# Modulation of the second block's rows: from VectorE before the transposes to ScalarE in the turned form

## The reference, cut to what matters

```python
def hybrid_layer(x, c_act, norm_g, w_ada, b_ada, w_in, w_out, pos):
    mod = c_act @ w_ada + b_ada
    shift, scale, gate = jnp.split(mod, 3, axis=-1)
    h = rms_norm(x, norm_g) * (1.0 + scale[:, None, :]) + shift[:, None, :]
    proj = h @ w_in
    ...                       # retention and stick-breaking attention of proj -> y
    return x + gate[:, None, :] * (y @ w_out)
```

## Time and profile before

| | us |
|---|---|
| median of 3 runs (1628.9 to 1629.87) | 1628.91 |
| the profiled execution, device time | 1628.01 |
| its span, first to last instruction | 1626.2 |
| TensorE busy in the span | 1583.9 (97%) |
| VectorE busy | 1069.6 (66%) |
| ScalarE busy | 728.7 (45%) |
| granted TensorE clock, mean over the span | 0.995 |

### The profile page before, as it was taken

How to read it: one execution, slowest core, us unless ns; L and a number is a source line. 1 busy time by engine, 2 the same in 40 slices (tenths; PEclk the granted TensorE clock), 3 DMA queues, 4 the chain that set the end, 5 groups by cost and what they waited for, 6 DMA issues and landing times.

```text
span 1626.2 us, 20209 instructions
## 1 busy us (share of the span) xinstructions
PE 1583.9 (97%) x8388; PEld 1327.8 (82%) x8388; DVE 1069.6 (66%) x1454; ACT 728.7 (45%) x874; POOL 48.9 (3%) x89
## 2 busy tenths in 40 slices
PE   7999999999989999999999999999999999999998
PEld 5898888888878888888888888788888878887986
DVE  5784776747666776575766746957767577556744
ACT  4545444433443443345444443454444344554452
POOL 1100000000000000000000000000100000000000
PEclk9999999999999999999999999999999999999999
DMA  8752466654424766452466654423766636433530
GB/s 268 257 184 77 156 227 251 241 224 177 160 78 169 281 224 252 149 208 83 164 240 237 257 197 163 155 79 127 272 257 233 229 133 225 145 129 117 207 117 26
DMA packets 45035, 299.89 MB, mean 184 GB/s; under 512 B 5444, under 2 KB 5700, under 8 KB 11280
## 3 DMA queue, kind: packets, MB, share of 16 engines
q1 hardware_dynamic: 38736, 278.48, 46.3%
q0 software_dynamic: 5776, 19.01, 3.8%
q10 hardware_dynamic: 432, 1.11, 0.2%
HBM read 296.20 MB, written 2.65 MB: 184 GB/s over the span
## 4 chain that ended last, share of the span: by engine, by line
PE 87%; DVE 8%; issue 2%; DMA 2%; ACT 1%; POOL 0%; SPq 0%; POOLq 0%; DVEq 0%; ACTq 0%
PE psum L925 25%; PE psum L927 25%; PE psum L926 25%; DVE w_low L1421 3%; PE psum L948 3%; PE psum L1139 2%; PE psum L1004 2%; DMA w_raw<-in_weights 2%; PE psum L1151 1%; PE psum L1065 1%; PE psum L1119 1%; PE psum L1203 1%; DVE arena L1703 1%; DVE work L1645 0%; DVE top L1642 0%
## 5 line engine op out<-in xcount | busy, mean ns | idle before, releaser
L925 PE MATMUL psum<-w_high,xt_high 128*128 128x512 f32 (+2 forms) x1472 | 576.5, 392 | 13.8 <-DVE w_low L1421 4.0
L1421 DVE TENSOR_TENSOR w_low<-w_raw,w_high 128x2048 fp32r<-128x2048 f32 x241 | 546.6, 2271 | 51.0 <-ACT w_high L1248 49.6
L1248 ACT ACTIVATE w_high<-w_raw 128x2048 fp32r<-128x2048 f32 x241 | 458.8, 1905 | 255.3 <-DMA w_raw<-in_weights 153.0
L927 PE MATMUL psum<-w_high,xt_low 128*128 128x512 f32 (+2 forms) x1472 | 566.7, 385 | 0.0
L926 PE MATMUL psum<-w_low,xt_high 128*128 128x512 f32 (+2 forms) x1472 | 565.8, 384 | 0.0
L925 PEld LDWEIGHTS psum<-w_high,xt_high 128*128 128x128 f32 x1472 | 278.7, 189 | 71.2 <-DVE w_low L1421 6.3
L927 PEld LDWEIGHTS psum<-w_high,xt_low 128*128 128x128 f32 x1472 | 278.4, 189 | 55.9
L926 PEld LDWEIGHTS psum<-w_low,xt_high 128*128 128x128 f32 x1472 | 279.0, 190 | 51.3
L1714 DVE TENSOR_TENSOR arena<-arena,psum 128x256 f32<-128x256 f32 x88 | 36.9, 420 | 205.5 <-ACT arena L1339 205.0
L925 PE MATMUL psum<-w_high,ht_high 128*128 128x512 f32 x352 | 140.8, 400 | 0.0
L927 PE MATMUL psum<-w_high,ht_low 128*128 128x512 f32 x352 | 137.5, 391 | 0.0
(11 more groups left out here) (225 smaller groups left out, 1605.3 us busy)
## 6 DMA issues: line engine op xcount, KB each, us to landing
w_raw<-in_weights SPq DMA_DIRECT2D x263, 1024.0 KB, 4.8
norm_params<-in_ln_g POOLq DMA_DIRECT2D x8, 512.0 KB, 4.3
norm_params<-in_ln_b POOLq DMA_DIRECT2D x8, 512.0 KB, 5.7
kv_outside<-arena POOLq DMA_DIRECT2D x3, 512.0 KB, 5.1
mem_kv<-kv_outside POOLq DMA_DIRECT2D x3, 512.0 KB, 3.6
norm_params<-mods_outside POOLq DMA_DIRECT2D x3, 512.0 KB, 5.8
x_rows<-in_x SPq DMA_DIRECT2D x2, 512.0 KB, 8.8
w_raw<-in_weights SPq DMA_DIRECT2D x2, 512.0 KB, 6.3
```

Of the source, the lines that this page charges most:

```text
L925: e.matmul(dst, a_hi, b_hi, start=first, stop=False)
L927: return e.matmul(dst, a_lo, b_hi, start=False, stop=last)
L1248: e.activation(K.w_hi[:, g % RING, 0:w], K.w_raw[:, r, 0:w], ACT.Copy).then_inc(K.high.hit(t), 1)
L1421: e.tensor_tensor(K.w_lo[:, s, 0:w], K.w_raw[:, r, 0:w], K.w_hi[:, s, 0:w].bitcast(F32), ALU.subtract).then_inc(K.taken.hit(t), 1)
```

## The change

- `modulate` moves to ScalarE and only scales the row by r: two copies of 512 columns with the scale column (semaphore `scaled`). In turned form a column of x is a partition, so gain and shift are then columns of 128 values. ScalarE's `xt` for ("sin", layer) makes, per group, four Identity activations of 128x128 with a bias and a scale column into `rows_turned`, waits for them, and rounds that to xt_high; VectorE's xt_low reads `rows_turned`. The others' `xt` are as before.
- `rms` squares in two halves of 512 columns, each behind its own half of x, and the scale 1/1024 goes into the square.
- gain and shift are loaded as columns (4 KB in runs of 4 bytes, four DMAs for the two layers) into a free buffer, so the waits of layer 1's load and of the decay's load go.
- The last down product of row block 1 in the last feed-forward is issued in two parts (one chunk of the depth each, 6 matmuls): part, group 0 of the turned rows 0, part, group 1. The `high` and `low` steps around it are put in another order.
- In layer 1, rows 1 are turned one product earlier (behind the fourth). In the output projection, rows 0 of the next layer are turned behind the second product of row block 1, not the third, and add_gated comes ahead of `split` in `last`.

```diff
@@ -199,12 +199,16 @@
...
-    def gemm(self, t, rb, half, gen, ring, use, kind="block", prompt=False):
+    def gemm(self, t, rb, half, gen, ring, use, kind="block", prompt=False, part=None):
+        if part == 0:
+            self.add("gemm", Gemm(t, rb, half, gen, ring, use, kind, part))
+            return
         for r in range(RB) if kind in BOTH else (rb,):
...
         self.last[t] = rb
-        self.add("gemm", Gemm(t, rb, half, gen, ring, use, kind))
+        self.add("gemm", Gemm(t, rb, half, gen, ring, use, kind, part))
         self.used[t] = self.used.get(t, 0) + 1
...
@@ -512,23 +516,29 @@
...
             for step in steps:
+                if rb and step == FF_STEPS - 1 and layer == LAST:
+                    down(step, t[step], rb, True, 0)
+                    self.xt(("sin", 0), 0, (0,))
+                    down(step, t[step], rb, True, 1)
+                    self.xt(("sin", 0), 0, (1,))
+                    self.ahead()
+                    continue
                 down(step, t[step], rb, True)
...
                         turn(FF_STEPS - 1)
-                elif step == FF_STEPS - 1:
-                    if layer == LAST:
-                        self.next_rows(layer, 0)
                 elif layer == LAST:
                     self.last_downs(step)
-                else:
+                elif step < FF_STEPS - 1:
                     if step == FF_STEPS - 2:
...
             if rb and layer == LAST:
+                self.low()
+                self.ahead()
                 self.low()
...
@@ -543,13 +553,12 @@
...
-        if step == FF_STEPS - 3:
+        if step == FF_STEPS - 4:
+            self.ahead()
+        elif step == FF_STEPS - 3:
+            self.add("rms", (0, 0))
+            self.add("modulate", (0, 0))
             self.low()
-            self.add("rms", (0, 0))
-            self.ahead()
-            self.add("modulate", (0, 0))
-        else:
-            self.ahead()
...
@@ -818,7 +827,12 @@
...
             self.on()
-        self.group([proj(0), proj(1)], gen, [[self.split] * 3 + [rotations(0), rows], [self.on] * 3 + [rotations(1), self.on]],
+        def rows_rotations():
+            late()
+            rotations(0)()
+        first = [rotations(0), rows] if layer == 0 else [rows_rotations, self.on]
+        self.group([proj(0), proj(1)], gen, [[self.split] * 3 + first, [self.on] * 3 + [rotations(1), self.on]],
                    layer == 0, proj(2))
...
@@ -869,19 +883,21 @@
...
         def turned():
-            self.low()
             if layer + 1 < DEPTH_2:
                 self.xt(("sin", layer + 1), 0)
-            else:
+            self.split()
+        def third():
+            if layer + 1 == DEPTH_2:
                 self.add("final", 0)
...
         def last():
+            added(3)
             self.split()
-            added(3)
         self.group([("w_out_2", layer, h * BLK, "half", sums(h)) for h in range(2)], mix,
-                   [[self.split, self.split, first, second], [self.split, self.split, turned, last]], True)
+                   [[self.split, self.split, first, second], [self.split, turned, third, last]], True)
...
@@ -995,7 +1011,7 @@
...
         elif stage == "sin":
-            pe.wait_ge(*K.modulated.at((j.gen[1], rb, g)))
+            pe.wait_ge(*K.scaled.at((j.gen[1], rb, g)))
             src = K.rows2[:, rb, :]
...
@@ -1014,12 +1030,12 @@
...
             pe.wait_ge(*K.tr.out(plan.ff_turn[j.gen[1], j.half]))
-            for h in range(2):
-                for c in range(2):
-                    left = [v[:, c, rb * P:rb * P + P] for v in (K.ht_hi[j.half % 4], K.ht_lo[j.half % 4])]
-                    w = c * D + h * BLK
-                    m = products(e, psum[:, K.wide.place(j.use) + h, :], left[0], left[1], hi[:, w:w + BLK],
-                                 lo[:, w:w + BLK], first and c == 0, last and c == 1)
+            parts = (0, 1) if j.part is None else (j.part,)
+            for h, c in ((h, c) for h in range(2) for c in parts):
+                left = [v[:, c, rb * P:rb * P + P] for v in (K.ht_hi[j.half % 4], K.ht_lo[j.half % 4])]
+                w = c * D + h * BLK
+                m = products(e, psum[:, K.wide.place(j.use) + h, :], left[0], left[1], hi[:, w:w + BLK],
+                             lo[:, w:w + BLK], first and c == 0, last and c == 1)
         else:
...
@@ -1253,9 +1270,20 @@
...
         act.wait_ge(*K.turned.at(j.use))
-        e.activation(hi[:, 4 * j.g:4 * j.g + 4, j.rb * P:j.rb * P + P],
-                     psum[:, K.tr.place(j.use), :].rearrange("p (c s) -> p c s", s=P),
-                     ACT.Copy).then_inc(K.xt_high.hit(j.use), 1)
+        src = psum[:, K.tr.place(j.use), :].rearrange("p (c s) -> p c s", s=P)
+        at = (slice(None), slice(4 * j.g, 4 * j.g + 4), slice(j.rb * P, j.rb * P + P))
+        if j.gen[0] == "sin":
+            act.wait_ge(*K.ld_gain2.at(j.gen[1]))
+            act.wait_ge(*K.ld_shift.at(j.gen[1]))
+            shift, gain = K.mod_cols[j.gen[1]]
+            for c in range(4):
+                k = 4 * j.g + c
+                m = e.activation(K.rows_turned[j.g][:, c, :], src[:, c, :], ACT.Identity, bias=shift[:, k:k + 1],
+                                 scale=gain[:, k:k + 1])
+            m.then_inc(K.modulated.hit(j.use), 1)
+            act.wait_ge(*K.modulated.at(j.use))
+            src = K.rows_turned[j.g]
+        e.activation(hi[at], src, ACT.Copy).then_inc(K.xt_high.hit(j.use), 1)
...
@@ -1356,12 +1384,21 @@
...
         layer, rb = j
-        if layer == 0:
-            act.wait_ge(*K.biased.at((("ln2", LAST), rb, 1)))
-        else:
-            act.wait_ge(*K.gated.at((layer - 1, rb, 1)))
-        e.activation(K.rows2[:, rb, :], K.x[:, rb, :], ACT.Square,
-                     accum_out=K.expsum[:, rb, 0:1]).then_inc(K.squared.hit(j), 1)
+        for n in range(2):
+            cols = slice(n * BLK, n * BLK + BLK)
+            act.wait_ge(*(K.gated.at((layer - 1, rb, n)) if layer else K.biased.at((("ln2", LAST), rb, n))))
+            m = e.activation(K.rows2[:, rb, cols], K.x[:, rb, cols], ACT.Square, scale=D ** -0.5,
+                             accum_out=K.expsum[:, rb, n:n + 1])
+        m.then_inc(K.squared.hit(j), 1)
+    def modulate(j):
+        layer, rb = j
+        act.wait_ge(*K.inverse_root.at((("rms", layer), rb)))
+        act.wait_ge(*K.squared.at(j))
+        for n in range(2):
+            cols = slice(n * BLK, n * BLK + BLK)
+            e.activation(K.rows2[:, rb, cols], K.x[:, rb, cols], ACT.Copy,
+                         scale=K.rstd[:, rb, 0:1]).then_inc(K.scaled.hit((layer, rb, n)), 1)
...
@@ -1444,8 +1481,10 @@
...
         v.wait_ge(*K.xt_high.at(j.use))
-        e.tensor_tensor(lo[at], psum[:, K.tr.place(j.use), :].rearrange("p (c s) -> p c s", s=P), hi[at].bitcast(F32),
-                        ALU.subtract).then_inc(K.tr.sem(j.use), 1)
+        src = psum[:, K.tr.place(j.use), :].rearrange("p (c s) -> p c s", s=P)
+        if j.gen[0] == "sin":
+            src = K.rows_turned[j.g]
+        e.tensor_tensor(lo[at], src, hi[at].bitcast(F32), ALU.subtract).then_inc(K.tr.sem(j.use), 1)
...
@@ -1755,20 +1794,8 @@
...
         v.wait_ge(*K.squared.at(j))
-        e.tensor_scalar(K.rstd[:, rb, 0:1], K.expsum[:, rb, 0:1], 1.0 / D, EPS_2, ALU.mult,
+        e.tensor_scalar(K.rstd[:, rb, 0:1], K.expsum[:, rb, 0:1], K.expsum[:, rb, 1:2], EPS_2, ALU.add,
                         ALU.add).then_inc(K.variance.hit((("rms", layer), rb)), 1)
-    def modulate(j):
-        layer, rb = j
-        v.wait_ge(*K.inverse_root.at((("rms", layer), rb)))
-        for h in range(2):
-            row = K.rows2[:, rb, halves[h]]
-            v.wait_ge(*K.ld_gain2.at(layer))
-            e.scalar_tensor_tensor(out=row, in0=K.x[:, rb, halves[h]], scalar=K.rstd[:, rb, 0:1],
-                                   in1=K.gain_row[:, halves[h]], op0=ALU.mult, op1=ALU.mult).then_inc(K.stepped.hit(), 1)
-            v.wait_ge(*K.ld_shift.at(layer))
-            v.wait_ge(*K.stepped.now())
-            e.tensor_tensor(row, row, K.shift_row(layer)[:, halves[h]], ALU.add).then_inc(K.modulated.hit((layer, rb, h)), 1)
...
@@ -1950,7 +1977,6 @@
...
         pool.wait_ge(*K.mods_stored[1].at(0))
-        pool.wait_ge(*K.modulated.at((0, 1, 1)))
         e.dma_start(K.decay, T["decay"]).then_inc(K.ld_decay.hit(0, 16), 16)
...
@@ -1966,15 +1992,15 @@
...
+    def modulation_columns(layer, part):
+        return K.mods_outside[layer].rearrange("(a b) c -> a (b c)", b=2)[part].rearrange("(k p) -> p k", p=P)
     def load_modulation(layer):
         pool.wait_ge(*K.mods_stored[layer].at(0))
-        if layer == 0:
-            pool.wait_ge(*K.tr.out(plan.units[LAST, 1][-1].out))
-        else:
-            pool.wait_ge(*K.biased.at((("ln2", LAST), 1, 1)))
-            pool.wait_ge(*K.modulated.at((layer - 1, 1, 1)))
-        e.dma_start(K.shift_row(layer), modulation_row(layer, 0)).then_inc(K.ld_shift.hit(layer, 16), 16)
```

(14 more changed lines are left out.)

21 lines of the change are left out of this document (10 added, 11 removed).

## The result

The changed kernel took 1634.14 us (median of 7 runs, 1633.25 to 1637.21), the kernel before 1627.87 beside it (7 runs, 1626.28 to 1629.87): ratio 1.0036, 95% interval 1.0026 to 1.0045. Timed twice more beside the experiments it came to 1.0024 (1.0013 to 1.0035) and 1.0028 (1.0018 to 1.0038). So it is slower by 4 to 6 us. The prediction had +4.0 us, a median of 1632.9, with a range of 1628.0 to 1636.5.

What follows compares the result with a forecast made beforehand. TensorE, busy 97% of the span, was taken as the bound, so only what holds or slows it counts. Terms 0.9 + 1.5 + 1.25 - 0.45 + 0.75 = +4.0 us on 1628.9 gave 1632.9, range 1628.0 to 1636.5.

Steps and rivals of the forecast that it cites:

- Size of the Identities: ScalarE's four Identity activations per group of turned chunks: taken as 1.5 us, with bounds 0.8 and 1.85.
- First place, rows 0: Second block's first turn: VectorE's chain, and the fifth product behind turned rows 0, come later by +0.9 us.
- First place, rows 1: Turn behind the fifth product: transposes to next product hold four Identities more, +1.5 us, bubble 2.9 us for 1.3.
- Second place, rows 0: Layer 1's first product: PSUM bank free 1.15 us later, as add_gated follows xt_low and a low part on VectorE.
- Second place, rows 1: Layer 1: 1.07 us bubble won, but the rotation now stands behind xt_low on VectorE, +1.25 us.
- Tail: End of the kernel: final square in halves, its first half beside the last product, -0.45 us.
- Clock: TensorE: old slow stretch stays; the new 2.9 us gap brings another with half weight, +0.75 us.
- Loads: Column loads replacing row broadcasts, issued long ahead of use: taken as costing nothing.
- Rival C: Column loads hold up weight tiles beside transfers at 1346 to 1370 us; 1637 if one is 4 us late; chance 0.07.
- Rival A: ScalarE's Identities are cheap, four in 0.8 us: sum -0.85, time 1628.1, not slower; chance 0.37.
- Rival B: Both new TensorE gaps, 2.9 and 2.2 us, fall to the slow clock: 1635.2 us; chance 0.14.

Runs made afterwards that it cites:

- low_after_power: Changed kernel with VectorE waiting for GpSimd's power before it makes the low part of a weight tile; ratio 1.0016 to the kernel before.
- low_beside_power: Kernel before with halved squares and the second place's new order, plus weight low parts moved beside GpSimd's power at the first place; ratio 0.9987.
- whole_product: Changed kernel with the last down product in one piece and the turn of rows 0 behind it; ratio that of the changed kernel.
- the repeat: The changed kernel timed and profiled again without edit, beside the first experiments; ratio 1.0024 to the kernel before.
- no_identity: Changed kernel without the four Identity activations per group, so gain and shift are not applied in the second block; ratio 0.9973 to the kernel before.

## Why the prediction was right, step by step

- **Size of the Identities**: predicted x = 1.5 us. ScalarE's timeline of the changed kernel, four Identities and the Copy behind them:

```profile
1328.97 1.51 ACT L1281 ACTIVATE arena<-psum,mem_kv 128x128 f32<-128x128 f32 x4
1330.51 0.63 ACT L1286 ACTIVATE xt_high<-arena 128x512 fp32r<-128x512 f32 x1
```

  1.51 us; one Identity takes 0.454 us on the mean of 32, where 0.465 was put: the price of a second column, inferred from one priced column in the earlier trace rows, was right. By the Trainium skill, "ScalarE: Activation LUTs", section "What ACT_TABLE_LOAD costs", it was to be 1.64, an estimate; the trace is 0.13 under it.
- **First place, rows 0**: predicted +0.9 at VectorE's chain and at G5, measured +2.14 (1333.84 - 2.22 - 1329.48). This is the term that was mis-sized. The step that failed is "POOL takes 0.56": it was taken from the kernel before, in which nothing stood beside this power, while the same paragraph of the prediction moved W2's low part there. low_after_power and low_beside_power show it, and with the short power the term is +0.98. The power grew by 1.97 us and G1 came 1.2 us later; the other 0.8 us were hidden, since the transposes of rows 0 would have waited for the product's first half.
- **First place, rows 1**: predicted +1.5, a bubble of 2.9 us. The bubble is 2.64 for 1.07, but it cost nothing: the product behind it stands at +2.14, as G5 does. The +1.5 was a sum with a G5 that stays slow. whole_product, where G5 was slow, has it: 8.11 us from G5 to that product (1342.93 to 1351.04), for 6.55 in the kernel before. In the three profiles of the changed kernel G5 was fast, and there are 6.54 or 6.55 us.
- **Second place, rows 0**: predicted +1.15 at the bank; measured a wait of 2.24 us for 0.92, and from the turn of rows 1 to layer 1's first product +1.25 in the repeat (3.40 - 2.15). The view names w_low L1458 as releaser, but it ended at 1483.21, when add_gated began; the bank came 0.69 us later: the wait of before under another name. The second product's wait of 0.57 us, which the prediction had kept, does not show, because the slow stretch at the first product runs over it: in whole_product, where that stretch did not come, the second product waits 0.60 us.
- **Second place, rows 1**: predicted no bubble and +1.25 at the rotation in place of the +1.15, so +0.1 more; measured no wait for xt_low, 1.12 at the rotation, and +0.90 more in the repeat. The rotation's transposes in the kernel before, and in the repeat:

```profile
1495.04 0.60 PE L1065 MATMUL psum<-ident,arena 128*128 128x128 f32 x4
...
1501.33 0.66 PE L1082 MATMUL psum<-ident,arena 128*128 128x128 f32 x4 [1.15 <-DVE arena L1603]
```

- **Tail**: predicted -0.45, measured -0.32 (-0.34 in the repeat): from last matmul to the span's end 8.16 us for 8.48.
- **Clock**: predicted that G5's slow stretch stays and that half a new one comes behind rows 1's turn, +0.75. G5's stretch went in all three profiles of the changed kernel; one behind rows 1's turn came in one of three; and one that was not forecast came in layer 1 in all three. The last makes its product 1.6 us longer in the repeat (4.42 for 2.84) and costs 0.76: from layer 1's first product to the rotation are 20.43 us in the repeat (1480.90 to 1501.33) and 19.67 in whole_product (1480.74 to 1500.41), where it did not come. The failed step is the reading by a stall's length: one of 1.77 us preceded a slow stretch in the kernel before and none in the changed one, and the 2.64 us one did so once in three.
- **Loads**: predicted nothing, and no tile waits. Rival C falls, and by its premise too: the queue q0 has 5,328 packets for 5,776. Four broadcasts of 512 KB went and four column loads came, and the profile's count of packets under 512 B rose by 64 (5,508 for 5,444), so 16 packets a load and not 1,024. The prediction took C's premise from a rule on descriptors; the trace counts packets, and does not show how many descriptors one holds.

The repeat, in which no slow stretch came at the first place, between checkpoints:

```
                                          predicted   repeat
to G5                                      +0.9        +2.16
to the product behind rows 1's turn        +1.5        -0.01
slow stretch behind it (half of 1.5)       +0.75        0
to the first product of layer 1            +1.15       +1.25
to the rotation's transposes               +0.1        +0.90
to the last matmul                          0          +0.05
tail                                       -0.45       -0.34
sum                                        +4.0        +4.0
```

So the +4.0 holds and the Identities' price and the waits of layer 1 are as forecast, but the first place adds up by luck: the power is 1.25 us that the prediction lacks, and the slow G5 that did not come took 1.5 us off rows 1. The clock's +0.75 came as 0.76 at another place. Rival A (x = 0.8) falls by the rows; its direction was right in no_identity. Rival B was seen in one execution only: both stretches, +7.0. What the prediction did not see at all is that the order and the halves, taken alone, win 3.6 us (0.22% of 1629) over the kernel before, in an order near the change's: it priced each of them only beneath the Identities.

## What to carry to other kernels

A step moved to an engine that has time is still paid in latency where the end waits for its result: four small instructions, 1.5 us in a row, stood in each way from transposes to product, and outweighed 10 us of relieved VectorE. When an instruction is moved, read what it will run beside as well as what it stands in front of. And price the by-parts of a change alone: here the reordering and the halved squares made the fastest kernel that computes the reference (1625.25 us) once the main part was left out. And a slow stretch or a wait is only worth what the next checkpoint moves by: G5's slow product was 1.5 us longer and cost 0.07 us, because what came behind it waited for VectorE in any case.
